# Where SyncE issues the modulation tiles among the weight tiles of a two-layer decoder trunk

## What is computed

```python
cond = jax.nn.silu(c)
for layer in range(DEPTH):                       # 2
    mod = cond @ ada_w[layer] + ada_b[layer]     # (2048,) @ (2048, 12288)
    sh1, sc1, g1, sh2, sc2, g2 = jnp.split(mod[:, None, :], 6, axis=-1)
    h = rms_norm(x) * (1.0 + sc1) + sh1
    y = even_mixer(...) if layer % 2 == 0 else odd_mixer(...)
    x = x + g1 * y
    h = rms_norm(x) * (1.0 + sc2) + sh2
    gate, up = jnp.split(h @ ffn_w_in[layer], 2, axis=-1)
    x = x + g2 * ((jax.nn.silu(gate) * up) @ ffn_w_out[layer])
return rms_norm(x, final_norm)
```

## Time and profile before

| what | us |
|---|---|
| median of 3 runs | 2250.82 (2249.72 to 2250.97) |
| the profiled execution | 2253.35 |
| its span, first to last instruction | 2251.6 |
| TensorE busy in the span | 2158.6 (96%) |
| VectorE busy | 1622.1 (72%) |
| ScalarE busy | 970.7 (43%) |
| granted TensorE clock, mean | 0.991 of full speed |
| moved by DMA | 594.08 MB, mean 264 GB/s |

### The profile page before, as it was taken

How to read it: one execution, slowest core, us unless ns; L and a number is a source line. 1 busy time by engine, 2 the same in 40 slices (tenths; PEclk the granted TensorE clock), 3 DMA queues, 4 the chain that set the end, 5 groups by cost and what they waited for, 6 DMA issues and landing times.

```text
span 2251.6 us, 26205 instructions
## 1 busy us (share of the span) xinstructions
PE 2158.6 (96%) x9996; PEld 1786.9 (79%) x9996; DVE 1622.1 (72%) x1690; ACT 970.7 (43%) x1271; POOL 9.9 (0%) x22
## 2 busy tenths in 40 slices
PE   3789999989999999999999999989999999999998
PEld 2678888768888888888887888878888888888886
DVE  5988898897789988777767665587665554555455
ACT  4344444454443334434445444454443344434443
POOL 0000000000000000000000000000000000000000
PEclk9899999999999999999999999999999999999999
DMA  9968877769888999977755533347765555555543
GB/s 390 421 279 315 331 299 318 300 287 367 326 325 351 378 386 385 385 280 284 284 213 232 197 126 117 122 187 295 285 247 203 199 191 186 186 190 197 192 149 149
DMA packets 82446, 594.08 MB, mean 264 GB/s; under 512 B 9296, under 2 KB 9328, under 8 KB 10672
## 3 DMA queue, kind: packets, MB, share of 16 engines
q1 hardware_dynamic: 81072, 588.29, 67.8%
q0 software_dynamic: 1280, 4.51, 0.7%
HBM read 590.66 MB, written 2.10 MB: 263 GB/s over the span
## 4 chain that ended last, share of the span: by engine, by line
PE 83%; DVE 9%; DMA 4%; ACT 2%; DVEq 1%; issue 1%; SPq 0%; ACTq 0%
PE ps L1308 25%; PE ps L1310 25%; PE ps L1309 25%; DVE w_lo L773 3%; PE ps L1296 3%; DVE ada_raw L777 2%; DMA gate<-in_ada 2%; DMA raw<-in_ffn_out 1%; PE ps L1391 1%; ACT w_hi L467 1%; DVE gate L777 1%; PE ps L1390 1%; PE ps L1324 0%; PE ps L1409 0%; PE ps L1408 0%
## 5 line engine op out<-in xcount | busy, mean ns | idle before, releaser
L773 DVE TENSOR_TENSOR w_lo<-raw,w_hi 128x1024 fp32r<-128x1024 f32 x728 | 881.3, 1224 | 478.3 <-ACT w_hi L467 474.0
L467 ACT ACTIVATE w_hi<-raw 128x1024 fp32r<-128x1024 f32 x728 | 762.6, 1060 | 991.5 <-PE ps L1310 794.6
L1308 PE MATMUL ps<-w_hi,xT_hi 128*128 128x512 f32 x1952 | 776.1, 398 | 36.4 <-DVE xT_lo L1026 26.7
L1310 PE MATMUL ps<-w_hi,xT_lo 128*128 128x512 f32 x1952 | 767.2, 393 | 0.0
L1309 PE MATMUL ps<-w_lo,xT_hi 128*128 128x512 f32 x1952 | 766.5, 393 | 0.0
L1308 PEld LDWEIGHTS ps<-w_hi,xT_hi 128*128 128x128 f32 x1952 | 370.8, 190 | 115.3 <-DVE xT_lo L1026 29.0
L1310 PEld LDWEIGHTS ps<-w_hi,xT_lo 128*128 128x128 f32 x1952 | 370.5, 190 | 79.1
L1309 PEld LDWEIGHTS ps<-w_lo,xT_hi 128*128 128x128 f32 x1952 | 371.3, 190 | 75.3
L777 DVE SCALAR_TENSOR_TENSOR ada_raw<-ada_raw,cond 128x2048 f32<-128x2048 f32 x176 | 402.3, 2286 | 17.4 <-DMA ada_raw<-in_ada 16.3
L1308 PE MATMUL ps<-w_hi,hT_hi 128*128 128x512 f32 x896 | 351.8, 393 | 4.6 <-DVE gate L805 1.6
L1310 PE MATMUL ps<-w_hi,hT_lo 128*128 128x512 f32 x896 | 349.0, 390 | 0.0
(11 more groups left out here) (169 smaller groups left out, 928.8 us busy)
## 6 DMA issues: line engine op xcount, KB each, us to landing
ada_raw<-in_ada SPq DMA_DIRECT2D x176, 1024.0 KB, 6.4
raw<-in_ffn_in SPq DMA_DIRECT2D x176, 1024.0 KB, 4.9
raw<-in_ffn_out SPq DMA_DIRECT2D x88, 1024.0 KB, 4.9
raw<-in_ab_in SPq DMA_DIRECT2D x48, 1024.0 KB, 8.4
raw<-in_swa_in SPq DMA_DIRECT2D x20, 1024.0 KB, 4.9
raw<-in_ab_out SPq DMA_DIRECT2D x16, 1024.0 KB, 8.1
raw<-in_swa_out SPq DMA_DIRECT2D x16, 1024.0 KB, 4.8
spare<-in_ada SPq DMA_DIRECT2D x8, 1024.0 KB, 8.2
```

Source lines behind the costliest of these rows:

```text
L467: nc.scalar.activation(w_hi[:, p % PAIRS, :, :], raw[:, t % RAW, 2 * (p % 2):2 * (p % 2) + 2, :], ACT.Copy).then_inc(hi_ready, 1)
L773: tt(w_lo[:, p % PAIRS, :, :], raw[:, (p // 2) % RAW, 2 * (p % 2):2 * (p % 2) + 2, :], w_hi[:, p % PAIRS, :, :].bitcast(F32), ALU.subtract ...
L1308: mm(out, hi[:, kt, tok], w_hi[:, q % PAIRS, k, :], start=(kt == 2 * ps0), stop=False)
L1310: last = mm(out, lo[:, kt, tok], w_hi[:, q % PAIRS, k, :], start=False, stop=(kt == 2 * ps1 - 1))
```

## The change

Tiles keep their slots, their order among each other and their waits, and VectorE's, ScalarE's and TensorE's programs stay as they are. Only SyncE's order changes. What was `ada_after` is now `ada_due`. The new `ada_after(t)` returns what was due `late` quads ago, where `late` is 2 in stages of more than 3 quads and 1 in others. Behind the last quad of a stage (or of one iteration of a loop) it returns all that is left, which are the tiles due after the last three quads. Every stage with tiles has at least 6 quads, so `late` is 2 in all of them.

```diff
     def ada_after(self, t):
+
+        late = 2 if self.quads > 3 else 1
+        due = range(t - late, t - late + 1) if t < self.quads - 1 else range(t - late, t + 1)
+        return [a for u in due if u >= 0 for a in self.ada_due(u)]
+
+    def ada_due(self, t):
 
         n, skip = 2 * self.ada, self.lag // 2
         if t < skip:
```

## The result

The kernel became slower: 2256.61 us median of 9 runs (2253.45 to 2258.66) against 2250.97 of 9 runs of before, ratio 1.0021 with a 95% interval of 1.0012 to 1.0029. I had forecast 2247.2 and a range up to 2252.0. The profiled execution has a span of 2255.1 us, 3.5 more than before's 2251.6. The medians lie 5.6 us apart: the profiled execution of before was 2.4 us above its median, that of after 0.3, so the traces show less than the whole loss.

A forecast was written before the change was run, and what follows sets the result against it. TensorE, busy 2158.6 of 2251.6 us, was taken as the bound; AB_OUT's 2.6 plus the first FFN-out's 1.0 made 3.6 us, so 2250.8 - 3.6 = 2247.2 us, own range 2246.4 to 2249.1, 8-in-10 range 2244.8 to 2252.0.

The forecast's parts named there:

- What bounds the kernel: Whole kernel: TensorE busy 2158.6 us of a span of 2251.6, so DMA order can win at most 93 us.
- AB_OUT: AB_OUT stage: VectorE's waits of 3.42 us shrink to 0.8, a gain of 2.6 us, between 1.7 and 3.4.
- the gate wait: In AB_OUT, TensorE's wait for VectorE's gate copy (L805), forecast to be gone; TensorE's waits there total 5.6 us.
- the 0.18 us: In AB_OUT, VectorE's wait of 0.18 us tied to late weights 13, forecast to go.
- What the change moves: SyncE's queue: weights gain a quad of lead (5.4 us), tiles leave at the same point of VectorE's work.
- AB1, AB23 and the rest: Other stages: TensorE's waits (1.1 us for L973, 0.4) come from VectorE's own queue, no DMA in front; gain 0.
- The cover: Thin stages: VectorE's lead over TensorE, 8.6 us, covers tiles that lose lead, so their lateness costs nothing.
- Rival 3: Iteration heads: a three-transfer burst makes VectorE stand in AB_OUT and the first FFN-out; net 5.5 us slower, 2256.3; chance 0.12.
- The rule of the Trainium skill: DMA queues: descriptors are consumed in ring order, so weights sent ahead hold a tile back; costed at 0.8 us in AB_OUT.
- The first FFN-out: End of layer 0's first FFN-out: TensorE's 1.0 us wait at 744.67 goes; gain 1.0 us, bounds 0 and 1.0.
- The thin stages: Stages with 6 or 4 tiles for 8 quads: tiles lose lead, down to three pairs (8.2 us), costed at nothing.
- Rival 1: Dense stages: bandwidth is the limit and order is worth nothing; 0 to 1 us gained, 2250.3; chance 0.18.

The follow-up runs named there:

- the run with AB_OUT alone: Late order (two quads) in AB_OUT only, every other stage in the order of before, against before: 2248.62 us, ratio 0.9989.
- the run with AB1 and AB23 alone: Late order in AB1 and AB23 only, every other stage in the order of before, against before: 2255.26 us, ratio 1.0016.
- the run with `lag`: After's order of DMAs, with VectorE taking AB23's tiles from pair 5 on (lag=4), against before: 2259.77 us, ratio 1.0033.
- tile 0 first: As after, but tile 0 of every iteration leaves behind weights 0 again, weights 1 and 2 behind it, against before: 2257.19 us, ratio 1.0027.

## Why the prediction was wrong, step by step

**What bounds the kernel** was right, and so was AB_OUT: 2.6 us forecast, 2.4 in the profile of after, 2.9 by medians in the run with AB_OUT alone, whose interval goes from 0.5 to 4.5. Weights 7 left at 396.16, which is the forecast 392 with TensorE 4.1 us late. The wait for them, the gate wait and the 0.18 us went as told; of the waits for tiles 1.3 us stayed in place of 0.8. TensorE kept waiting 0.91 us before pair 16, as L1112 still came last.

**The step that failed** stands in "What the change moves": "the tiles leave at the same point of VectorE's work as before". They do leave there (289.10 and 289.11), but I took the time of issue for the time of landing. In AB_OUT I counted the transfers in front of tile 10; for the other stages with a tile for each quad I stopped at the issue and wrote "AB1, AB23 and the rest" with 0 behind it. In place of this 0 stood 4.6 us for AB23 in the trace of after, 3.6 by the ratio of the run with AB1 and AB23 alone, and in the FFN 2.2 us in the trace where the sum had 1.0 won. The same count, applied to AB23, would have given tile 0 at 300.3 (it was used at 299.3) against the 295.75 at which VectorE wanted it.

**The cover was the wrong one.** I covered late tiles with VectorE's lead of 8.6 us, which is the lead of `w_lo` over the matmuls. It doesn't hold for what TensorE gets from VectorE without four buffers between: in AB23 it transposes the softmax weights at a fixed pair, and VectorE was only 0.8 us ahead with them. VectorE is 0.91 busy there (54.5 of the 60 us from 255 to 315 before), so it has little room to catch up. And in the FFN the 8.6 us didn't suffice for `w_lo` itself, where a late tile and a block of the residual came together: TensorE waited 1.18 and 1.14 us.

**Rival 3** had the burst behind the last quad and the size, 5.5 us slower at 2256.3 against 2256.61 measured. That the number agrees is luck, for its places were wrong. I priced weights 0 of the next iteration, which had their old lead, and AB_OUT and the FFN-out. The victims were the tiles behind the burst, and 4.6 us of the loss fell in AB23, which I hadn't named. AB_OUT, which it had losing 2.7, won. And it had 0.12 where its own line in the profile, engines 0.99 busy, called for more: a full queue is the case in which an earlier weight has to push something back.

**The rule of the Trainium skill** that I weighed (DMA: Bandwidth & Descriptors, "Queues, rings and completion order": descriptors are consumed in ring order) was the one that decided, and I let it cost 0.8 us in one stage. The traces agree with it: transfers end where a count in order of issue puts them, within 1.0 us at 299.3 and 760.0, and within 0.4 at 305.6, 714.8 and, in the run with `lag`, 310.4.

**The first FFN-out.** The wait at 744.67 did go, and between 730 and 745 TensorE won back 1.3 us, but the second iteration's tiles had cost 1.7 before, and the next head cost 1.7 more. The term of 1.0 in the sum was wrong besides: it was sized from a wait that four of five other traces with the order of before in the FFN don't show, so the order had nothing to win there. The thin stages cost nothing, as told: VectorE waits 1.8 us for a tile once (512.9) and then up to 0.5 us at a time in the first FFN-in after, and TensorE never does.

**Rival 1** was half right. In the dense stages bandwidth was full, and order still mattered, for the worse.

## What to carry to other kernels

In a DMA queue that is served in order and is nearly full, an earlier issue for one stream is a later landing for the other: here tile 0, issued at 289.1 in both kernels, was used at 295.75 in one and had landed at 299.3 in the other, with the DMA engines 0.99 busy (290 to 315 in before). Count each stream's landing (transfers in front times the time of one) against the moment it is wanted, at the place with the least time to spare, in every stage and not only in the one where the gain is expected. Buffer depth covers only consumers that stand behind the buffers; for a hand-over without them, look for its own slack. And don't size a gain from a wait of 1 us in one trace: look whether other executions have it.

## What the runs showed of the hardware

- **A short wait costs more than itself.** TensorE stood 2.58 us for L973, and from 318 to 321 it ran at the lower of its two clocks. Stretches after: us, busy by engine (count), granted clock, DMA share, GB/s.

```profile
314.00:318.00 4.00, 1.42 (x9) 0.92 (x8) 3.41 (x12) 4.00 (x6) 0.00 (x0) 1.00 0.01 6
318.00:321.00 3.00, 3.00 (x10) 2.13 (x9) 3.00 (x4) 0.59 (x2) 0.00 (x0) 0.50 0.39 112
322.00:326.00 4.00, 4.00 (x20) 3.27 (x19) 3.86 (x6) 1.31 (x2) 0.00 (x0) 1.00 1.02 432
```

  0.50 of full speed is 1.2 of 2.4 GHz. The wait of 1.57 us of the earlier trace rows was followed by no such stretch. In the other traces waits of 2.66 and 2.05 us (AB1 and AB23 alone, at 318 and 430), of 2.93 (tile 0 first, at 316) and of 2.55 (`lag` with after's order, at 368) were followed by one, and the 1.97 at 341 of the last was not. That the wait caused the drop is the order of the rows; no run tests it. A wait costs more than itself without the drop too: those of 0.94 and 1.01 us for the softmax cost TensorE 1.7 us at the full clock.
- **The low stretch at a norm falls here or there.** At norm 3 before, the 1.2 GHz stretch lay on the first matmuls behind the wait of 3.1 us; after, it lay on the transposes ahead of it, which took 3.60 us in place of 1.97, and the wait was 1.45. TensorE came out 1.4 us earlier for it, but 12 us later it waited 0.67 us for `w_lo`, as before did not, and 0.9 of the 1.4 was gone. The first lines are of before, the second of after.

```profile
1505.28 1.97 PE L1296 MATMUL ps<-ident,work 128*128 128x128 f32 x16 [1.79 <-DVE work L833]
1510.33 0.76 PE L1308 MATMUL ps<-w_hi,xT_hi 128*128 128x512 f32 x1 [3.08 <-issue]
```

```profile
1509.26 3.60 PE L1302 MATMUL ps<-ident,work 128*128 128x128 f32 x16 [1.78 <-DVE work L839]
1514.31 0.47 PE L1314 MATMUL ps<-w_hi,xT_hi 128*128 128x512 f32 x1 [1.45 <-issue]
...
1526.11 0.47 PE L1314 MATMUL ps<-w_hi,xT_hi 128*128 128x512 f32 x1 [0.67 <-DVE w_lo L779]
```

  It goes either way in kernels whose instructions are the same there: at norm 2 four of the traces are 1.6 us earlier than before's for it, and the others within 0.3. So it can be part of why single executions of one kernel spread by 5 us and more; how large a part isn't shown.
